# A three-stage FFN entry: the first group computed as token rows, and small reorderings where stages meet

## The reference, cut to what matters

```python
def rmsnorm(x, g):
    y = x * rsqrt(mean(x * x, -1) + 1e-6)
    return y * g

def swiglu(x, w_gate, w_up, w_down):                 # ffn0, ffn1
    return (silu(x @ w_gate) * (x @ w_up)) @ w_down

def conv_ffn(u, w_up, conv_w, conv_b, w_down):       # ffn2, ffn3
    hdn = causal_dwconv(u @ w_up, conv_w) + conv_b   # 3 taps along the tokens
    gate, val = split(hdn, 2)
    return (silu(gate) * val) @ w_down

h = h + 0.5 * swiglu(rmsnorm(h, g1), ...)            # ffn0
h = h + mixer(rmsnorm(h, gm)) @ w_out                # mix0, mix0o
h = h + 0.5 * swiglu(rmsnorm(h, g2), ...)            # ffn1
h = h + sigmoid(rmsnorm(h, g3) @ w_ple) * emb        # ple
for layer in (0, 1):                                 # ab / abo / ffn2, then hg / hgo / ffn3
    h = h + rmsnorm(mixer(rmsnorm(h, a)), b)
    h = h + rmsnorm(conv_ffn(rmsnorm(h, c), ...), d)
```

## Time and profile before

| | us |
|---|---|
| median of 3 runs | 1299.86 |
| the profiled execution | 1299.16 |
| its span, first to last instruction | 1297.3 |
| PE busy | 1257.2 (97%) |
| DVE busy | 852.8 (66%) |
| ACT busy | 664.2 (51%) |
| mean granted TensorE clock | 0.992 |

### The profile page before, as it was taken

The page is one execution under the profiler, slowest core; times in us unless marked ns, Lnnn a source line. Parts: engine busy times, 40 slices in busy tenths (PEclk is TensorE's granted clock), DMA queues, the critical chain, the costliest instruction groups (busy, mean ns, idle before and its releaser), DMA issues. The chain is left out here.

```text
span 1297.3 us, 21437 instructions
## 1 busy us (share of the span) xinstructions
PE 1257.2 (97%) x8591; PEld 1153.8 (89%) x8591; DVE 852.8 (66%) x1126; ACT 664.2 (51%) x954; POOL 53.3 (4%) x77
## 2 busy tenths in 40 slices
PE   5999999998999999999999999999999999999997
PEld 5999998887999998799988899999799887999996
DVE  4545557787644445747867766666878867666666
ACT  4533446464544334646521655444777546544554
POOL 5000000010000000101300000000000000000000
PEclk8999999999999999999999999999999999999999
DMA  9965555324556653653221555555443334455520
GB/s 298 315 194 181 180 175 163 131 72 156 185 189 195 194 189 106 195 179 129 100 66 45 180 183 172 184 194 195 162 163 130 131 96 164 163 195 195 194 98 33
DMA packets 139419, 209.76 MB, mean 162 GB/s; under 512 B 9924, under 2 KB 101314, under 8 KB 139344
## 3 DMA queue, kind: packets, MB, share of 16 engines
q1 hardware_dynamic: 136080, 198.86, 46.3%
q0 software_dynamic: 2976, 9.26, 2.5%
q10 hardware_dynamic: 288, 0.59, 0.1%
HBM read 207.64 MB, written 1.05 MB: 161 GB/s over the span
## 5 line engine op out<-in xcount | busy, mean ns | idle before, releaser
L278 DVE TENSOR_TENSOR wlo<-raw,whi 128x1024 fp32r<-128x1024 f32 x380 | 446.2, 1210 | 114.7 <-ACT whi L273 114.4
L286 PE MATMUL psum<-xh,whi 128*128 128x256 f32 x1704 | 484.9, 285 | 5.7 <-DVE wlo L278 4.7
L287 PE MATMUL psum<-xl,whi 128*128 128x256 f32 x1704 | 483.7, 284 | 0.0
L288 PE MATMUL psum<-xh,wlo 128*128 128x256 f32 x1704 | 483.6, 284 | 0.0
L273 ACT ACTIVATE whi<-raw 128x1024 fp32r<-128x1024 f32 x380 | 379.5, 1042 | 115.0 <-PE psum L288 104.5
L286 PEld LDWEIGHTS psum<-xh,whi 128*128 128x128 f32 x1704 | 327.9, 192 | 9.3 <-issue 6.9
L287 PEld LDWEIGHTS psum<-xl,whi 128*128 128x128 f32 x1704 | 327.9, 192 | 1.6
L288 PEld LDWEIGHTS psum<-xh,wlo 128*128 128x128 f32 x1704 | 327.8, 192 | 0.2
L286 PE MATMUL psum<-whi,hidh 128*128 128x512 f32 x352 | 137.9, 392 | 2.4 <-DVE hidl L833 2.4
L286 PE MATMUL psum<-whi,xh 128*128 128x512 f32 (+2 forms) x328 | 129.5, 395 | 8.5 <-DVE xl L309 3.6
L287 PE MATMUL psum<-wlo,hidh 128*128 128x512 f32 x352 | 137.4, 390 | 0.0
(11 more groups left out here) (314 smaller groups left out, 1063.3 us busy)
## 6 DMA issues: line engine op xcount, KB each, us to landing
raw<-in_ffn_w_up SPq DMA_DIRECT2D x132, 512.0 KB, 5.0
raw<-in_ffn_w_down SPq DMA_DIRECT2D x88, 512.0 KB, 4.4
raw<-in_ffn_w_gate SPq DMA_DIRECT2D x44, 512.0 KB, 4.0
raw<-in_c_w_in SPq DMA_DIRECT2D x32, 512.0 KB, 4.5
raw<-in_ab_w_in SPq DMA_DIRECT2D x28, 512.0 KB, 4.7
raw<-in_w_in SPq DMA_DIRECT2D x18, 512.0 KB, 4.5
raw<-in_w_out SPq DMA_DIRECT2D x8, 512.0 KB, 4.0
raw<-in_ple_w_gate SPq DMA_DIRECT2D x8, 512.0 KB, 4.2
```

The lines of the kernel that those rows point to most:

```text
L278: nc.vector.tensor_tensor(lo, r, hi.bitcast(F32), ALU.subtract).then_inc(lo_done, 1)
L286: nc.tensor.matmul(pe_out, sh, mh, start=start, stop=False, skip_group_check=True)
L287: nc.tensor.matmul(pe_out, sh, ml, start=False, stop=False, skip_group_check=True)
L288: return nc.tensor.matmul(pe_out, sl, mh, start=False, stop=stop, skip_group_check=True)
```

## The change

Five things are changed.

1. `ROWS_FIRST`: at the entries of ffn1, ffn2 and ffn3 the first group of 256 gate and 256 up columns is computed as token rows (the tokens stationary, 512 weight columns moving) into bank 0 for tile 0 and bank 1 for tile 1. `piece(t, k)` is then 6 matmuls of 512 columns of one tile and one piece. Three of tile 0's four pieces come before tile 1's inputs are waited for, two of them before tile 1's transposes. ACT copies bank 0 and DVE bank 1 to `first_rows` (new lines 788 and 794), PE transposes the eight blocks back into the usual layout (new line 803) after the first piece of group 1, and `act_hidden` of group 0 waits for that. Pieces 2 and 3 are cut at another place in ACT's and DVE's order, and the zeroing of banks 0 to 3 comes after piece 2 of group 1.
2. The zero products go from 16 to 0 at ffn1's entry, from 22 to 8 at those of ffn2 and ffn3 (now ahead of the first row product), and from 22 to 18 at hg's.
3. `act_first_half`: the first tiny step of `act_rstd` (line 460 before) is issued right after the first half's squares. In stages after a norm of their own, both gain products of tile 1 come before its additions.
4. The convolution of ffn2 and ffn3 goes by halves (gate, then up), each in a bank of its own, so that silu of the gate half may run beside the up half.
5. At the end of ffn2 and ffn3, piece 13 is cut on ACT ahead of silu and on DVE after the low part of the hidden tile, and tile 0 takes the last two pieces in the order piece by piece.

```diff
-        IDLE_TURN = {"ffn1": 13, "ffn2": 20, "hg": 20, "ffn3": 20}
-        IDLE_TURNED = {"ffn1": 3, "ffn2": 2, "hg": 2, "ffn3": 2}
+        IDLE_TURN = {"ffn1": 0, "ffn2": 8, "hg": 16, "ffn3": 8}
+        IDLE_TURNED = {"hg": 2}
...
+            if X in ROWS_FIRST:                       # pe_between
+                pe_idle_products(pe, IDLE_TURN[X], 4)
+                pe.wait_ge(*after(f"{X}.xl00"))
+                piece(0, 0)
+                piece(0, 1)
+                pe_turn_second(pe, X)
+                pe.wait_ge(*after(f"{X}.xl01"))
+                piece(0, 2)
+                wait_turned(pe, X, 0)
+                piece(1, 0)
+                piece(1, 1)
+                piece(0, 3)
+                wait_turned(pe, X, 1)
+                piece(1, 2)
+                piece(1, 3)
+                return
...
+                if b == 0 and prev != "ple":          # act_between, after squares(t, b)
+                    act_first_half(act, X, "ss", t)
...
             if X:
+                if X in ROWS_FIRST:
+                    first_pieces(split_hi, act, X, (2, 3))
                 turn(1, 0)
                 turn(1, 1)
...
                 product_gain(1, 0)                    # dve_between, after a norm
+                product_gain(1, 1)
                 add(1, 0)
-                product_gain(1, 1)
                 add(1, 1)
...
                 add(1, 0)                             # dve_between, else
+                turn(0, 0)
                 add(1, 1)
-                turn(0, 0)
-            if X:
+            if X in ROWS_FIRST:
+                turn(0, 1)
+                normed(1, 0)
+                normed(1, 1)
+                first_pieces(split_lo, dve, X, (2,))
+                turn(1, 0)
+                turn(1, 1)
+                first_pieces(split_lo, dve, X, (3,))
+            elif X:
...
-            order += [(0, b, n) for b in range(2) for n in rest]
+            order += [(0, b, n) for n in rest for b in range(2)] if X in ("ffn2", "ffn3") else [(0, b, n) for b in range(2) for n in rest]
...
+        def gate_or_up(n, q, j, c):
+            return psum[:, 4 + 2 * q + c, 256 * j:256 * j + 256] if n < 2 else psum[:, 4 + 2 * q + j, 256 * c:256 * c + 256]
+        def pe_rows_piece(pe, n, t, k):
+            p = 2 * first_slot[X] + k
+            pe.wait_ge(lo_done, p + 1)
+            for kk in range(2):
+                kc = 2 * k + kk
+                last = three(bank(t), xh[:, kc, tok], xl[:, kc, tok], wh[:, kk, :], wl[:, kk, :], start=(kc == 0), stop=(kc == KC - 1))
+            if t == 1:
+                last.then_inc(used, 1)
+            elif k == 3:
+                last.then_inc(*steps.did("pe", f"{X}.row0"))
+        def act_first_row(act, n):
+            act.wait_ge(*after(f"ffn{n}.row0"))
+            nc.scalar.activation(first_rows[:, 0, :], bank(0), ACT.Copy)
+        def dve_first_row(dve, n):
+            dve.wait_ge(used, 2 * first_slot[f"ffn{n}"] + 4)
+            nc.vector.tensor_copy(first_rows[:, 1, :], bank(1))
+        def pe_rows_turn(pe, n):
+            for t in range(NT):
+                pe.wait_ge(*after(f"ffn{n}.copied{t}"))
+                for j in range(2):
+                    for c in range(2):
+                        last = nc.tensor.transpose(gate_or_up(n, 0, j, c)[:, t * P:t * P + P], first_rows[:, t, col:col + P], ident)
...
+            if first and f"ffn{n}" in ROWS_FIRST:     # act_hidden
+                act.wait_ge(*after(f"ffn{n}.columns"))
...
-            last.then_inc(conv_mid, 1)
-            act.wait_ge(conv_all, g + (G0 - 2 * GROUPS) + 1)
+                last.then_inc(conv_mid, 1)            # now once for each j
+            if last_piece is not None:
+                split_hi(act, last_piece)
+            act.wait_ge(conv_all, 2 * g + 2 * (G0 - 2 * GROUPS) + 1)
...
             dve_hidden(dve, n, g, 0, 0)               # dve_ffn, last group
-            tail_splits(13)
+            if n < 2:
+                tail_splits(13)
             dve_hid_lo(dve, n, g, 0)
+            if n >= 2:
+                tail_splits(13)
...
-        LATE = {"x": (0, 1, 2, 3), "mix0o": (2, 3), "abo": (2, 3), "ffn2": (2, 3), "hgo": (2, 3)}
+        LATE = {"x": (0, 1, 2, 3), "ffn2": (2, 3)}
```

More of the change, by code:

```diff
@@ L334, in build @@
         TILE_FIRST = ("mix0", "ple", "ab")
+        ROWS_FIRST = ("ffn1", "ffn2", "ffn3")
         BANKS = [(t, b) for t in range(NT) for b in range(2)]
@@ L453, in wait_h, with act_first_half @@
                 eng.wait_ge(*after(f"{prev}.h{t}{b}"))
+        def act_first_half(act, part, ss, t):
+            total, r = row_sums(part)
+            act.wait_ge(*after(f"{part}.{ss}{t}0"))
+            nc.scalar.activation(r[:, t:t + 1], total[:, 2 * t:2 * t + 1], ACT.Identity, bias=eps_col)\
+                .then_inc(*steps.did("act", f"{part}.{ss}m{t}"))
         def act_rstd(act, part, ss, t):
@@ L458, in act_rstd @@
             m = r[:, t:t + 1]
-            act.wait_ge(*after(f"{part}.{ss}{t}0"))
-            nc.scalar.activation(m, total[:, 2 * t:2 * t + 1], ACT.Identity, bias=eps_col).then_inc(*steps.did("act", f"{part}.{ss}m{t}"))
             act.wait_ge(*after(f"{part}.{ss}{t}1"))
@@ L615, in pe_between @@
                 return
-            if piece:
+            if piece and X not in ROWS_FIRST:
                 if X == "ab":
@@ L755, in pe_ffn @@
             p = 2 * first_slot[X]
-            pe_between(pe, X)
-            pe_gate_up(pe, n, 0, 0, p, 0)
-            for b in range(4):
-                nc.tensor.matmul(bank(b), zero_r[:, :], xh[:, 0:2, :], start=True, stop=True, skip_group_check=True)
+            early = {}
+            if X in ROWS_FIRST:
+                pe_between(pe, X, lambda t, k: pe_rows_piece(pe, n, t, k))
+                early = {0: lambda: pe_rows_turn(pe, n), 2: lambda: pe_zero_sums(pe)}
+            else:
+                pe_between(pe, X)
+                pe_gate_up(pe, n, 0, 0, p, 0)
+                pe_zero_sums(pe)
             def body(i):
@@ L763, in body @@
                     q = p + 4 + 6 * half
-                    pe_gate_up(pe, n, i * 2 + half + 1, (half + 1) % 2, q, i)
+                    first = isinstance(i, int) and half == 0
+                    pe_gate_up(pe, n, i * 2 + half + 1, (half + 1) % 2, q, i, early if first else {})
                     pe_down(pe, n, i * 2 + half, half, q + 4, i)
@@ L808, in dve_hidden @@
                 return
[L809 to L814 removed]
+            for j in range(2):
+                count = 2 * g + 2 * (G0 - 2 * GROUPS) + j + 1
+                dve.wait_ge(conv_mid, count)
+                for k, done in ((1, conv_one), (0, conv_all)):
+                    if k == 0:
+                        dve.wait_ge(conv_one, count)
+                    lag = 2 - k
                     for c in range(2):
```

48 lines of the change are left out of this document (32 added, 16 removed).

## The result

The changed kernel takes 1286.78 us (median of 4 runs, 1285.21 to 1288.11) against 1299.83 of the kernel before (median of 4). The ratio is 0.990, 95% interval 0.9887 to 0.9913, that is 11.3 to 14.7 us less. The profiled execution took 1285.21 us, its span is 1283.4.

The account below looks back on a forecast made before the run. PE, busy 97% of the span, was taken as the bound. The sum 6.6 + 1.2 + 1.2 - 0.4 + 0.7 = 9.3 us off 1299.16 gave 1289.9 profiled, 1290.6 for the runs, range 1288.0 to 1295.6.

Parts of the forecast that it names:

- The entries (parts 1 and 2): Entries of ffn1, ffn2, ffn3: row form completes group 0 earlier, less 1.07 us of transposes back; 2.2 us each, 6.6 together.
- The start at 4.4 us: ffn2's entry: first row product about 4.4 us after tile 0's transposes start.
- the row products at 0.23 us each: Row form of group 0: a 512-column matmul starts every 0.23 us, 48 take 11.04, 0.55 us cheaper than before.
- hidden copies: ACT's and DVE's copies of the rows, 0.6 to 0.7 us each, hidden by 4 to 5 us.
- one us of cover: Group 0's hidden chain ends near 760.7 while PE finishes group 1 at 761.7, so PE would not wait.
- Part 3: Early tiny step and gain products first: 0 at ffn2's and ffn3's entries, 0.4 us lost at hg's, 0.7 gained at the end.
- hg's entry at a loss of 0.4: Tile 0's halves arrive 0.7 apart instead of 1.4, steps pile up: 0.4 us later, bounds 0 to 0.7.
- Parts 4 and 5: Ends of ffn2 and ffn3: `hidl` at least 1.3 us earlier, PE's wait goes; 1.2 us gained at each.
- The tails stay: Rival: cuts bind the last group, piece 13's low part is late, PE waits as before; 1292.6 us, chance 0.12.
- the rows give nothing: Rival: group 0's copies and chain come late, PE waits 2.2 us per entry; 1297.2 us, chance 0.12.
- The clock falls: Rival: falls of 1.7 us at entries with fewer fillers; four give 1297.4 us, eight 1304.2, chance 0.05 each.
- hg's entry not late and the norms earlier: Better outcome than the forecast, from hg's entry and the norms: 1288.5 us, chance 0.04.

Follow-up runs that it names:

- rows_only: Kernel before plus only the row form of the first group and fewer zero products: 1294.39 us, ratio 0.9947.
- after_no_half: Changed kernel with the root's first tiny step back behind both squares, both gain products still first: 1283.63 us, one execution.
- tail_only: Kernel before plus only the convolution by halves and the new order of piece 13 and tile 0's last products: 1297.14 us, ratio 0.9975.
- after_old_gain: Changed kernel with tile 1's second gain product back between the additions, the tiny step still early: 1288.53 us, one execution.
- after_no_halves: Changed kernel with the convolution whole again, new bank layout and piece 13's new place kept: 1287.34 us, one execution.
- after_no_fill: Changed kernel without any zero products at the entries of ffn2, hg and ffn3 (0 instead of 8, 18, 8): 1290.29 us, ratio 0.9936.

## Why the prediction was wrong

**The entries (parts 1 and 2): right.** Predicted 2.2 each; rows_only has 2.67, 2.30, 2.30. The start at 4.4 us (4.42), the row products at 0.23 us each (36 in 8.28) and the hidden copies came out as said. The 48 row products take 2.86 and 8.28 us, 11.14 in all against 11.59 of before: 0.45 saved by their form, where the prediction had 0.55. Two small errors nearly cancel. One is a price: the eight transposes back to columns take 0.80 us (749.16 to 749.96) and those of tile 1 0.88 (737.13 to 738.01), not the 1.07 read at an entry. The other is the wait of 0.4 at the first down product, where the prediction had one us of cover. In the changed kernel group 0's last row product ends 15.8 us after T, where the prediction had 16.6.

**Part 3: the step that failed.** The prediction said "both gain products of tile 1 now stand ahead; the same instructions have run by then, so it stays at about 736.1", priced the norms at 0 and hg's entry at a loss of 0.4. The same instructions had run, but the waits between them had gone. Before, DVE stood 0.35 us for the root with a gain product in hand that it could have done, and 0.10 for its own result; in the new order the product fills the wait. The other 0.2 us is overlap: two instructions on DVE that follow each other without a wait start 0.08 us before the one ahead ends, and the two that waited lost that. Together it is 0.64 us at ffn2's and at ffn3's first row product: 4.42 in rows_only, 3.78 in after_no_half, which has the new order without the early tiny step. (rows_only also lacks parts 4 and 5, but they leave the stretch from T to the first product alone: tail_only has 8.35 there, like the kernel before.) after_old_gain shows it the other way round: 4.27, so the tiny step by itself gives 0.15, and on top of it the order 0.49. The two do not add. The tiny step was priced at +0.2 where both halves are ready; at ffn2 its handovers are 0.03 and not 0.09 us, and the root is complete 4.72 us after T with it and 4.68 without. Mix0's entry pays 0.3 for it, and ffn2's end 0.13 (16.51 us in after_no_half). At hg's entry the two errors make 1.0 us: -0.4 predicted, +0.6 measured. At the end 0.95 instead of 0.7.

**Parts 4 and 5: the right sum from the wrong parts.** Predicted 1.2 at each end, half from the halves and half from piece 13. Measured 1.39 and, with part 3's 0.95 taken off, 1.5 to 1.6. In the changed kernel the halves alone are enough for all of it; piece 13 and the new order bring nothing at ffn3's end and cost 0.2 at ffn2's. With the convolution whole, part 5 is not idle: PE's wait for `hidl` is 0.5 us at the most in after_no_halves, where it was 1.2 at each end before. And the halves do a second thing that the prediction called free: they shorten group 0's chain by the 0.4 us that PE would otherwise wait at each conv entry.

**The rivals.** "The tails stay" and "the rows give nothing" did not come. "The clock falls" did not come either, but after_no_fill shows that it would have with the last fillers gone. The fillers taken away at ffn1, ffn2 and ffn3 were not needed: idle stretches of 0.2 to 0.65 us replaced them, and the granted clock is 1.00 at these entries in all three traces of the changed kernel. Small pauses thus did not decide here; those of 4.31 us and, once of twice, of 2.46 us did.

**The range.** By the distances the surplus of 4.3 us is 1.0 at hg's entry, 2.1 at the entries of ffn2 and ffn3, 0.7 at ffn1's, 0.8 at the two ends, less 0.3 at mix0's. All terms but mix0's erred to the same side. The largest share is part 3: 0.6 at each of ffn2's and ffn3's entries, the 1.0 at hg's and 0.25 at the end. The 0.4 of the halves at both conv entries is the next; the rest are handovers and short steps, each priced a little above what it took. The range had 2.6 us below the forecast and 5 above. The prediction did name this side, "hg's entry not late and the norms earlier", but gave it a chance of 0.04 and 2.1 us, where 3.8 came.

What stays open: why the clock falls at the places where PE is busy without a pause (near 560 us in all sixteen traces but one, near 616 us in all) was not tried.

## What to carry to other kernels

When an instruction is moved ahead of one that waits, price the wait that it fills, not only its length: the order of the instructions behind may be the same and the time still less. An instruction that waits also gives up its overlap with the one ahead. Read handovers between dependent instructions from the trace to 0.01 us when a chain has twenty of them; small amounts rounded to the same side add up over the entries of all stages. Work that fills a filler's place is worth more than the filler, but keep fillers where a pause of several us would remain.

## What the runs showed of the hardware that was not expected

- PE's clock falls in steps that cost 1.5 to 1.7 us each, at a handful of fixed places, but not in every execution. The three traces of the changed kernel hold three, three and four of them; a fall or two more or less is thus the size of the 3 us between runs of one kernel, though the unprofiled runs do not show their falls. A pause of 4.31 us brought a fall before it had ended (0.78 in the window of the pause, 0.50 for eight us after it); one of 2.46 us did at ffn3 and not at ffn2; the pauses of 1.97 us at hg's output product were followed by one in nine of thirteen traces, those of 1.89 us near 296 us in six of sixteen; pauses of 1.2 to 1.6 us, and of 0.6, by none. Near 560 and 616 us it fell with PE 100% busy in the windows around.
- The distance between two fixed points of a busy PE repeats to 0.01 us over 147 us (147.36 or 147.37 in fourteen of sixteen traces at ffn2; rows_only and after_no_halves, the two with the row form and the whole convolution, have 147.43 and 147.42), so one trace tells differences of 0.1 us where the medians of five runs tell 2 us.
- On DVE, an instruction of 128x512 float32 starts 0.08 us before the one ahead ends if it needs nothing from it, and 0.10 us after its end if it needs its result (733.92 + 0.69 to 734.71 before).
- Transposes of 128x128 float32 blocks start every 0.10 us back to back.
